# Two small reorderings in a two-block transformer kernel: where the short weight tile of the second output half stands, and when ScalarE splits the third weight tile of the convolutional FFN

## The chip, the cores and the metric

The kernel runs on one core of a Trainium2 chip. The metric is the device time of one execution in microseconds (us); lower is better. TensorE (PE in the profile) multiplies matrices, VectorE (DVE), ScalarE (ACT) and GpSimd (POOL) work on vectors, and SyncE (SP) issues the loads of the weights. Each engine runs its own instruction list in order and meets the others through semaphores.

## The reference, cut to what matters

The reference is two blocks of two layers each on 512 tokens (the first block also carries 256 context tokens in its first layer), in float32. The change touches the down projections of all four feed-forward networks, and the start of the two convolutional ones. Cut to these:

```
_swiglu(h, w_gate, w_up, w_down) = (silu(h @ w_gate) * (h @ w_up)) @ w_down   # first block, 2 layers

def conv_ffn(h, w_up, conv_w, conv_b, w_down):                                # second block, 2 layers
    u = h @ w_up
    u = sum(conv_w[2 - n] * shift(u, n) for n in range(3)) + conv_b           # along the tokens
    gate, up = split(u, 2, axis=-1)
    return (silu(gate) * up) @ w_down
```

The hidden width is 2816, that is 22 blocks of 128, and w_down is 2816 x 1024.

## The kernel before

**How a float32 product is made.** Each factor is held as a high part in the fp32r format and a low part, the rest of it. A product is three matmuls of 128x128 by 128x512 (`mm3`, lines 233 to 235): high by high, high by low, low by high.

**Weight tiles.** All weights pass through one numbered sequence of tiles. SyncE loads tile t into one of two raw buffers as soon as the low part of tile t-2 is made (line 394). ScalarE casts it to the high part (`ScalarLane.tile`, line 345; "hi" below), once TensorE has given back the buffer of tile t-2 (the key "used"). VectorE then makes the low part (`VectorLane.tile`, line 264; "lo"). Each call of `tile()` on ScalarE or VectorE makes sure that the tiles up to one ahead of TensorE's are made. Where the calls stand in the engines' own lists is written out by hand.

**Down projection.** `pe_out` computes the 1024 output columns in two halves of 512, half 0 over all 22 blocks and then half 1. `out_chunks` cuts each half into pieces of at most four blocks, so there are twelve chunks, numbered 0 to 11; 0 to 5 are half 0, 6 to 11 half 1. A chunk is one weight tile (4 blocks: 128x2048 values, 2 blocks: 128x1024). Half 0 is cut 4, 4, 4, 4, 4, 2, and half 1 is cut 4, 4, 2, 4, 4, 4. From the third chunk on TensorE takes one token tile after the other (nt of them: 6 in `down0`, 4 in `down1`, `cf_out0` and `cf_out1`), and for each the blocks of the chunk. So a chunk of n blocks is 3 x n x nt matmuls.

The activations of a chunk are split too: `act_chunk` copies each block of it to its high part (line 345, into rx), `dve_chunk` makes the low part (line 335), one block behind. TensorE waits for each block of the chunk.

VectorE's list, in `dve_out`, is for chunk c: the lo of tile c+1, the activations of chunk c+1, and, if c is the last chunk of a half, the outputs of that half from PSUM, token tile by token tile. So at the switch of the halves it is: lo of tile 6, activations of chunk 6, **outputs of half 0**, lo of tile 7, activations of chunk 7, lo of tile 8, and so on. In `down0` and `down1` an output is three operations (multiply by the gate at line 264, add the scaled residual at 274, statistics at 298); in `cf_out0` and `cf_out1` it is one addition (264). In `cf_out0` ScalarE also squares and sums the four outputs of half 0 (`act_flow_sums`), between the activations of chunk 6 and the hi of tile 7.

`down1` takes its last two chunks (10 and 11) interleaved by token tiles; this is the same in both kernels.

**Start of the convolutional FFN.** The up projection has 44 column tiles of 128 (n = 0 to 43), two per weight tile. Tiles n = 0 to 3 (weight tiles 0 and 1 of the stage) are computed by `pe_feat_halves`, first for tokens 0 to 255 and then for tokens 256 to 511, so all four end within a short stretch; TensorE then goes on with n = 4 and weight tile 2. For each n ScalarE copies the result from PSUM (line 345), VectorE makes three convolution operations on it (lines 270, 274, 274), and for the gate part (n = 0, 1, 4, 5, ...) ScalarE applies Silu (line 341). VectorE's list is: convolutions of n = 0 and 1, lo of weight tile 2, convolutions of n = 2 and 3, lo of weight tile 3. ScalarE's list before the change is: copy 0, Silu 0, copy 1, **hi of weight tile 2**, Silu 1, copy 2, copy 3, hi of weight tile 3.

Of the kernel before, what the change touches and what calls it, by code (L numbers as in the profile page):

```python
# [741 lines left out]

def out_chunks(Kn):


    cut = sorted({*range(0, min(Kn, 9), 4), *range(Kn, 7, -4)})
    return [(0, k0, min(4, Kn - k0)) for k0 in range(0, Kn, 4)] + [(1, i, j - i) for i, j in zip(cut, cut[1:])]


# [9 lines left out]
def out_order(Kn, nt, late):  # L759


    chunks = out_chunks(Kn)
    order = []
    for c, (h, k0, kn) in enumerate(chunks[:-2] if late else chunks):
        order += ([(c, k, t) for k in range(kn) for t in range(nt)] if c < 2 and h == 0 else
                  [(c, k, t) for t in range(nt) for k in range(kn)])
    if late:
        end = len(chunks)
        order += [(c, k, t) for ts in [(0, 1)] + [(t,) for t in range(2, nt)] for c in (end - 2, end - 1) for t in ts
                  for k in range(chunks[c][2])]  # L770
    return order


def pe_out(p, K, tag, W, Kn, nt, ready=None, between=(), chunks=False, turn=None, late=None):


    between, cut, ms, bs = dict(between), out_chunks(Kn), {}, {}
    order = out_order(Kn, nt, late)
    for i, (c, k, t) in enumerate(order):
# [32 lines left out]
def act_chunk(a, K, tag, c, Kn, nt, src, ready):  # L812
    h, k0, kn = out_chunks(Kn)[c]
    places = len(chunk_places(nt))
    if c >= places:
        a.wait_ge(*K.at(tag + "_used", c - places))
    for k in range(kn):
        a.wait_ge(*K.at(*ready, k0 + k))
        a.cp(chunk_parts(K, c, nt)[0][:, k, 0:nt * 128], src[:, k0 + k, 0:nt * 128]).then_inc(
            *a.sig((tag + "_chunk_hi", c, k)))  # L820
# [2655 lines left out]
def cf_out(K):  # L3476
    return K.mem(W1, 11264).rearrange("p (k n) -> p k n", n=512)
# [6 lines left out]
def cf_raw(K, n):  # L3484
    return K.mem(CF + 700 + n % 4 * 514, 514)


def cf_acc(K, n):
    return K.mem(CF + 2760 + n % 8 * 512, 512)


def cf_tiles():

    return [(f2 * 4 + part * 2 + f, part, f2 * 2 + f) for f2 in range(11) for part in range(2) for f in range(2)]
# [38 lines left out]
def act_conv_ffn(a, K, l):  # L3533
    a.wait_ge(*K.at("cf_edge", l))
    for n, part, ft in cf_tiles():
        if n % 2 == 0 and n > 2:
            a.tile()
        if n == 40:
            act_chunk(a, K, f"cf_out{l}", 0, 22, 4, cf_out(K), ("cf_GT", l))
        a.wait_ge(*K.at("cf", l, n))  # L3540
        if n >= 4:
            a.wait_ge(*K.at("cf_conv", l, n - 4))
        a.cp(cf_raw(K, n)[:, 2:514], K.ps("cf", l, n)[:, :]).then_inc(*a.sig(("cf_raw", l, n)))
        a.free("cf", l, n)
        if n == 1:
            a.tile()
        if part == 0:
            a.wait_ge(*K.at("cf_conv", l, n))
            a.act(cf_acc(K, n), cf_acc(K, n), ACT.Silu).then_inc(*a.sig(("cf_silu", l, n)))
# [593 lines left out]
def act_program(a, K):  # L4143
# [58 lines left out]
    yield "x0"  # L4202
    act_flow_halves(a, K, "nf0", K_FFN)
    act_conv_ffn(a, K, 0)
    first, second = act_flow_sums(a, K, "cf_out0", "nhg")
    act_out(a, K, "cf_out0", 22, 4, cf_out(K), ("cf_GT", 0), {5: first, 11: second}, 1)
# [8 lines left out]
    yield "x1"  # L4215
    act_flow_halves(a, K, "nf1", K_FFN + 8)
    act_conv_ffn(a, K, 1)
    act_out(a, K, "cf_out1", 22, 4, cf_out(K), ("cf_GT", 1), made=1)

# [227 lines left out]
```

## Time and profile before

| | |
|---|---|
| time, median of 3 runs | 4284.06 us (4283.25 to 4290.72) |
| the profiled execution | 4283.25 us, its span 4281.0 us |
| PE busy | 3910.1 us, 91% of the span |
| DVE busy | 2099.3 us, 49% |
| ACT busy | 1607.7 us, 38% |
| POOL busy | 561.9 us, 13% |
| mean granted clock of TensorE | 0.953 of full |

Times inside the execution are counted from the start of its span. A matmul's busy time in the profile overlaps that of the next one; the work that it costs is the distance between two starts. In the timeline, the bracket at the end of a row is the idle time of the engine just before the instruction and who ended it.

### The profile page before, as it was taken

Reading aid. Unit: us, or ns where it says so; the run is one execution under the profiler, and the core shown is the slowest. Engines: PE = TensorE matmul, PEld = TensorE weight load, DVE = VectorE, ACT = ScalarE, POOL = GpSimd, SP = SyncE. Lnnn points to the kernel's source line nnn. Section 1 sums busy time; section 2 is a strip of 40 time slices with the busy share of each in tenths; the row PEclk is TensorE's granted clock in tenths of the full one; section 3 lists DMA queues with packets and bytes.
Section 4 is the critical chain, followed back from the end, with each engine's and each line's share of the span. In section 5 each row is a group of like instructions: output and inputs, shape, how many; then the busy total and the mean of one; then the engine's idle time right before and its main releaser. Section 6 shows DMA issues by size and latency. Waiting matters only on the chain.

```text
span 4281.0 us, 67439 instructions
## 1 busy us (share of the span) xinstructions
PE 3910.1 (91%) x28266; PEld 3214.2 (75%) x28266; DVE 2099.3 (49%) x3022; ACT 1607.7 (38%) x2639; POOL 561.9 (13%) x628
## 2 busy tenths in 40 slices
PE   6978897878999998988899889989999998889999
PEld 4866685766888775756688776678888888678887
DVE  3545454656211363267423663554665428545564
ACT  3333333333111233155323335644334336544333
POOL 0035303642000001002100000000220003000220
PEclk8978898888999999999899999999999999999999
DMA  4234433131221121102232230131323230322232
GB/s 155 82 130 140 152 96 115 35 101 48 69 69 60 54 84 61 55 11 76 84 99 94 74 84 20 52 118 51 99 92 102 89 116 5 121 69 72 97 101 86
DMA packets 248535, 355.08 MB, mean 83 GB/s; under 512 B 9300, under 2 KB 158503, under 8 KB 247847
## 3 DMA queue, kind: packets, MB, share of 16 engines
q1 hardware_dynamic: 233840, 300.49, 21.7%
q0 software_dynamic: 13840, 50.11, 3.7%
q8 instruction: 222, 3.64, 0.4%
q14 instruction: 83, 0.67, 0.1%
q10 hardware_dynamic: 550, 0.17, 0.0%
HBM read 336.50 MB, written 14.24 MB: 82 GB/s over the span
## 4 chain that ended last, share of the span: by engine, by line
PE 76%; DVE 12%; ACT 7%; issue 2%; POOL 2%; DMA 1%; ACTq 0%; DVEq 0%; SPq 0%; POOLq 0%
PE psum L233 20%; PE psum L234 20%; PE psum L235 20%; PE psum L230 14%; ACT arena L341 3%; DVE arena L264 3%; PE psum L239 2%; DVE arena L274 2%; DVE rw L264 2%; DVE rx L335 2%; ACT arena L345 1%; POOL arena L379 1%; DVE arena L278 1%; ACT rw L345 1%; ACT rx L345 1%
## 5 line engine op out<-in xcount | busy, mean ns | idle before, releaser
L233 PE MATMUL psum<-rx,rw 128*128 128x512 f32 (+2 forms) x2864 | 1046.3, 365 | 53.7 <-DVE rx L335 27.7
L234 PE MATMUL psum<-rx,rw 128*128 128x512 f32 (+2 forms) x2864 | 1026.8, 359 | 0.0
L235 PE MATMUL psum<-rx,rw 128*128 128x512 f32 (+2 forms) x2864 | 1026.1, 358 | 0.0
L230 PE MATMUL psum<-arena 32*32 32x32 f32 (+10 forms) x12982 | 808.4, 257 | 159.3 <-ACT arena L345 64.5
L264 DVE TENSOR_TENSOR rw<-arena,rw 128x2048 fp32r<-128x2048 f32 (+2 forms) x239 | 537.6, 2249 | 829.8 <-ACT rw L345 824.1
L230 PEld LDWEIGHTS psum<-arena 32*32 32x32 f32 (+5 forms) x12982 | 612.8, 141 | 335.6 <-issue 118.6
L345 ACT ACTIVATE rw<-arena 128x2048 fp32r<-128x2048 f32 (+2 forms) x239 | 448.1, 1875 | 755.5 <-PE psum L235 728.9
L233 PE MATMUL psum<-rw,rx 128*128 128x512 f32 (+1 forms) x1720 | 682.0, 397 | 43.9 <-DVE rx L335 26.9
L234 PE MATMUL psum<-rw,rx 128*128 128x512 f32 (+1 forms) x1720 | 673.0, 391 | 0.0
L235 PE MATMUL psum<-rw,rx 128*128 128x512 f32 (+1 forms) x1720 | 672.7, 391 | 0.0
L233 PEld LDWEIGHTS psum<-rx,rw 128*128 128x128 f32 (+1 forms) x2864 | 548.5, 192 | 155.1 <-DVE rx L335 41.2
L234 PEld LDWEIGHTS psum<-rx,rw 128*128 128x128 f32 (+1 forms) x2864 | 549.9, 192 | 80.2 <-issue 4.1
L235 PEld LDWEIGHTS psum<-rx,rw 128*128 128x128 f32 (+1 forms) x2864 | 548.4, 191 | 78.5
L345 ACT ACTIVATE arena<-psum 128x512 f32<-128x512 f32 (+6 forms) x675 | 314.4, 466 | 757.3 <-PE psum L235 401.4
L379 POOL TENSOR_TENSOR arena<-arena 128x512 f32<-128x512 f32 (+5 forms) x300 | 420.2, 1401 | 969.5 <-DVE arena L274 389.5
L341 ACT ACTIVATE arena<-arena 128x512 f32<-128x512 f32 (+11 forms) x476 | 249.5, 524 | 471.5 <-DVE arena L274 219.3
L233 PEld LDWEIGHTS psum<-rw,rx 128*128 128x128 f32 x1720 | 327.7, 191 | 125.3 <-DVE rx L335 39.2
L235 PEld LDWEIGHTS psum<-rw,rx 128*128 128x128 f32 x1720 | 327.2, 190 | 68.4
L234 PEld LDWEIGHTS psum<-rw,rx 128*128 128x128 f32 x1720 | 327.8, 191 | 64.4
L274 DVE SCALAR_TENSOR_TENSOR arena<-arena 128x512 f32<-128x512 f32 (+8 forms) x481 | 353.9, 736 | 44.5 <-ACT arena L341 27.9
L264 DVE TENSOR_TENSOR arena<-arena,psum 128x512 f32<-128x512 f32 (+3 forms) x308 | 151.8, 493 | 311.5 <-PE psum L235 205.1
L239 PE MATMUL psum<-arena 128*128 128x128 f32 (+2 forms) x1284 | 196.0, 291 | 102.8 <-DVE arena L264 33.7
(71 smaller groups left out, 2092.5 us busy)
## 6 DMA issues: line engine op xcount, KB each, us to landing
arena<-in_ffn_w_up SPq DMA_DIRECT2D x66, 1024.0 KB, 5.1
arena<-in_ada_w SPq DMA_DIRECT2D x48, 1024.0 KB, 5.3
arena<-in_ffn_w_down SPq DMA_DIRECT2D x40, 1024.0 KB, 5.0
arena<-in_ffn_w_gate SPq DMA_DIRECT2D x22, 1024.0 KB, 5.2
arena<-in_dn_w_in SPq DMA_DIRECT2D x32, 512.0 KB, 5.4
arena<-in_xa_w_kv SPq DMA_DIRECT2D x16, 1024.0 KB, 5.0
arena<-in_hgrn_w_in SPq DMA_DIRECT2D x16, 1024.0 KB, 5.5
arena<-in_da_w_in SPq DMA_DIRECT2D x12, 1024.0 KB, 5.2
```

The source lines that it names most:

```text
L230: return self.e.matmul(out, l, r, start=start, stop=stop)
L233: self.e.matmul(out, l[0], r[0], start=start, stop=False)
L234: self.e.matmul(out, l[0], r[1], start=False, stop=False)
L235: return self.e.matmul(out, l[1], r[0], start=False, stop=stop)
L239: return self.e.transpose(out, a, self.K.ident[0:k, 0:k])
L264: return self.e.tensor_tensor(out, a, b, op)
L274: return self.e.scalar_tensor_tensor(out=out, in0=a, scalar=s, in1=b, op0=op0, op1=op1)
L278: return self.e.tensor_reduce(out, a, AX.X, op)
L335: return self.e.tensor_tensor(dst[1], src, dst[0].bitcast(F32), SUB)
L341: return self.e.activation(out, a, f, **kw)
L345: return self.e.activation(out, a, ACT.Copy, **kw)
L379: return self.e.tensor_tensor(out, a, b, op)
```

## The change

Two edits:

1. In `out_chunks` half 1 is cut 2, 4, 4, 4, 4, 4 instead of 4, 4, 2, 4, 4, 4. The number of chunks (twelve) and all other sizes stay. The short chunk of half 0 (chunk 5) is now followed by the short chunk of half 1 (chunk 6). For the other users of this function, with 8 blocks, both versions give 4, 4.
2. In ScalarE's list at the start of both convolutional FFNs the hi of weight tile 2 moves from behind copy 1 to behind Silu 1: copy 0, Silu 0, copy 1, Silu 1, **hi of weight tile 2**, copy 2, copy 3, hi of weight tile 3. VectorE's and TensorE's lists stay.

```diff
 def out_chunks(Kn):
-    cut = sorted({*range(0, min(Kn, 9), 4), *range(Kn, 7, -4)})
+    cut = [0] + list(range(Kn % 4 or 4, Kn + 1, 4))
     return [(0, k0, min(4, Kn - k0)) for k0 in range(0, Kn, 4)] + [(1, i, j - i) for i, j in zip(cut, cut[1:])]
...
 def act_conv_ffn(a, K, l):
     a.wait_ge(*K.at("cf_edge", l))
     for n, part, ft in cf_tiles():
-        if n % 2 == 0 and n > 2:
+        if n and n % 2 == 0:
             a.tile()
...
         a.cp(cf_raw(K, n)[:, 2:514], K.ps("cf", l, n)[:, :]).then_inc(*a.sig(("cf_raw", l, n)))
         a.free("cf", l, n)
-        if n == 1:
-            a.tile()
         if part == 0:
             a.wait_ge(*K.at("cf_conv", l, n))
             a.act(cf_acc(K, n), cf_acc(K, n), ACT.Silu).then_inc(*a.sig(("cf_silu", l, n)))
```

## Rows read from the trace of the kernel before

**Rows 1.** The page's shares of the chain that ended last, by engine.

```profile
PE 76%; DVE 12%; ACT 7%; issue 2%; POOL 2%; DMA 1%; ACTq 0%; DVEq 0%; SPq 0%; POOLq 0%
```

**Rows 2.** ACT timeline in `down0`, hi of tiles 6, 8, 11, 12: start us, us.

```profile
1496.64 1.92 ACT L345 ACTIVATE rw<-arena 128x2048 fp32r<-128x2048 f32 x1 [13.38 <-PE psum L235]
...
1521.12 1.06 ACT L345 ACTIVATE rw<-arena 128x1024 fp32r<-128x1024 f32 x1 [10.88 <-PE psum L235]
...
1564.66 1.92 ACT L345 ACTIVATE rw<-arena 128x2048 fp32r<-128x2048 f32 x1 [10.88 <-PE psum L235]
...
1580.98 1.92 ACT L345 ACTIVATE rw<-arena 128x2048 fp32r<-128x2048 f32 x1 [10.88 <-PE psum L235]
```

**Rows 3.** DVE timeline in `down0`: lo 5, activations of chunks 5 and 6, then lo 7.

```profile
1481.41 1.23 DVE L264 TENSOR_TENSOR rw<-arena,rw 128x1024 fp32r<-128x1024 f32 x1 [8.92 <-ACT rw L345]
1482.74 2.02 DVE L335 TENSOR_TENSOR rx<-arena,rx 128x768 fp32r<-128x768 f32 x2
...
1500.98 4.15 DVE L335 TENSOR_TENSOR rx<-arena,rx 128x768 fp32r<-128x768 f32 x4
...
1518.91 2.29 DVE L264 TENSOR_TENSOR rw<-arena,rw 128x2048 fp32r<-128x2048 f32 x1
```

**Rows 4.** Timeline of PE in `down0`, the first matmul of chunk 7.

```profile
1522.41 0.47 PE L233 MATMUL psum<-rw,rx 128*128 128x512 f32 x1 [1.39 <-DVE rx L335]
```

**Rows 5.** Timeline of ACT in `down1`, hi of tiles 6, 10 and 11.

```profile
2376.75 1.92 ACT L345 ACTIVATE rw<-arena 128x2048 fp32r<-128x2048 f32 x1 [8.37 <-PE psum L235]
...
2414.97 1.92 ACT L345 ACTIVATE rw<-arena 128x2048 fp32r<-128x2048 f32 x1 [0.86 <-PE psum L235]
...
2426.23 1.92 ACT L345 ACTIVATE rw<-arena 128x2048 fp32r<-128x2048 f32 x1 [6.68 <-PE psum L235]
```

**Rows 6.** DVE timeline in `down1`: activations of chunks 5 and 6, then lo 7.

```profile
2368.29 1.49 DVE L335 TENSOR_TENSOR rx<-arena,rx 128x512 fp32r<-128x512 f32 x2
...
2381.09 3.08 DVE L335 TENSOR_TENSOR rx<-arena,rx 128x512 fp32r<-128x512 f32 x4
...
2393.40 2.29 DVE L264 TENSOR_TENSOR rw<-arena,rw 128x2048 fp32r<-128x2048 f32 x1
```

**Rows 7.** Timeline of PE in `down1`, the first matmul of chunk 7.

```profile
2396.64 0.47 PE L233 MATMUL psum<-rw,rx 128*128 128x512 f32 x1 [3.26 <-DVE rx L335]
```

**Rows 8.** Timeline of ACT in `cf_out0`, hi of tiles 6 and 7.

```profile
3279.17 1.92 ACT L345 ACTIVATE rw<-arena 128x2048 fp32r<-128x2048 f32 x1 [8.37 <-PE psum L235]
...
3290.71 1.92 ACT L345 ACTIVATE rw<-arena 128x2048 fp32r<-128x2048 f32 x1
```

**Rows 9.** Timeline of PE in `cf_out0`, the first matmul of chunk 7.

```profile
3295.89 0.47 PE L233 MATMUL psum<-rw,rx 128*128 128x512 f32 x1
```

**Rows 10.** Timeline of ACT in `cf_out1`, hi of tiles 6 and 11.

```profile
4210.85 1.92 ACT L345 ACTIVATE rw<-arena 128x2048 fp32r<-128x2048 f32 x1 [8.37 <-PE psum L235]
...
4255.49 1.92 ACT L345 ACTIVATE rw<-arena 128x2048 fp32r<-128x2048 f32 x1 [7.04 <-PE psum L235]
```

**Rows 11.** Stretches for PE: us, PE busy (matmuls), granted clock, DMA share, GB/s.

```profile
1406.50:1417.90 11.40, 6.06 (x14) 0.70 0.27 93
2393.30:2401.00 7.70, 4.44 (x13) 0.78 0.42 136
3345.60:3351.60 6.00, 3.75 (x26) 1.00 0.01 3
```

**Rows 12.** Timeline of ACT at the first convolutional FFN's start.

```profile
3002.27 1.92 ACT L345 ACTIVATE rw<-arena 128x2048 fp32r<-128x2048 f32 x1
3004.37 0.63 ACT L341 ACTIVATE arena<-arena 128x512 f32<-128x512 f32 x1 [0.18 <-DVE arena L274]
```

**Rows 13.** Timeline of DVE there, lo of weight tile 2.

```profile
3004.44 2.29 DVE L264 TENSOR_TENSOR rw<-arena,rw 128x2048 fp32r<-128x2048 f32 x1
```

**Rows 14.** Timeline of PE there, last matmul of n = 3, first of n = 4.

```profile
3006.39 0.28 PE L235 MATMUL psum<-rx,rw 128*128 128x256 f32 x1
3006.79 0.50 PE L233 MATMUL psum<-rx,rw 128*128 128x512 f32 x1
```

## The prediction

> **What bounds the kernel now.** I read the page first: PE is busy 91% of the span and carries 76% of the chain that ended last [rows 1]. Neither edit adds or removes a matmul, a cast or a load, so only PE's waits can change. Then I read the timelines of ACT, DVE and PE side by side at the five kinds of place that the edits touch. The useful clock is ACT's hi cast: the hi of tile c+2 starts when TensorE gives back the buffer of chunk c, so its start marks the end of chunk c whenever the row names PE as releaser. I count tiles within a stage, as the chunks.
>
> The unit is a chunk. In `down0` two such marks are 1580.98 - 1564.66 = 16.32 us apart [rows 2]: four blocks by six token tiles by three matmuls, 72 in all, so 0.227 us a matmul. A block then costs 4.08 us of PE in `down0` and 0.227 x 12 = 2.72 us in the other three. The short chunk gives 8.16 us of cover in `down0` and 5.44 us elsewhere.
>
> From the end of chunk 4 to the end of chunk 9 both kernels work off 16 blocks. In `down0` this takes 1564.66 - 1496.64 = 68.02 us against 65.28, so 2.74 us are lost [rows 2]. In `down1`: 2426.23 - 2376.75 = 49.48 against 43.52, 5.96 lost [rows 5]. In `cf_out1`: 44.64 against 43.52, 1.12 lost [rows 10].
>
> The large loss is in chunk 7. DVE has just taken the outputs of half 0. In `down0` that is all between 1505.1, where the activations of chunk 6 end, and 1518.91, where the lo of tile 7 begins: 13.8 us for six outputs, 2.3 us each [rows 3]. The first matmul of chunk 7 starts at 1522.41, after 1.39 us of idleness put down to DVE [rows 4]. In `down1` it is four outputs, and PE idles 3.26 us [rows 7].
>
> **The change, part by part: the short chunk in place 6.** Two things move at the switch.
>
> *DVE's chain moves up.* Tile 6 and its activations are halved. In `down0` the hi takes 1.06 us instead of 1.92 [rows 2], the lo 1.23 instead of 2.29, the activations 2.02 instead of 4.15 [rows 3]. DVE has no gap from there to the lo of tile 7, so that comes 0.86 + 1.06 + 2.13 = 4.05 us earlier. In the stages with four token tiles the activations take 1.49 instead of 3.08 [rows 6], so it is 3.51 us earlier. The outputs can follow: PE finishes a token tile of chunk 5 every 1.36 us, DVE takes one every 2.3.
>
> *PE's cover shrinks* by 8.16 us, respectively 5.44. So PE waits longer before chunk 7, and what comes later has two blocks more to do. The first matmul of chunk 7 comes 4.05 (3.51) us earlier, and 8.16 (5.44) us of matmuls are moved behind it.
>
> `down0`: 8.16 - 4.05 = +4.11. The wait grows from 1.39 to about 5.4 us: chunk 6 ends at 1496.64 + 8.16 + 8.16 = 1512.96, the first matmul comes at 1522.41 - 4.05 = 1518.36. What does so long a pause do to the clock? At 1406.5 PE had paused 11.40 - 6.06 = 5.3 us and then ran 14 matmuls in 6.06 us, at a granted clock of 0.70 over the stretch. At full clock that is 3.17, so 2.9 us were lost. After the 3.26 us of `down1`, 13 matmuls took 4.44 us, so 1.5 lost. After 2.2 us at 3345.6 the clock stayed at 1.00 [rows 11]. So +2.9 here. Against that, chunk 7 now also loses about 1.1 us block by block, because DVE makes a block's low part in 4.15 / 4 = 1.04 us [rows 3] while PE uses it in 0.68; at the lower of the two clock levels, 1.2 GHz, PE takes 1.28, and this wait goes. Sum: 4.11 + 2.9 - 1.1 = **+5.9**.
>
> Here a rule stands beside the rows. The Trainium skill, page "TensorE: Matmul & The Clock Gate", section "Why this matters for your kernels", says that pauses between bursts of matmuls put the array back to its half rate, and that one should keep them short. The two longer pauses agree; the 2.2 us pause shows that not every pause does it here. Without the rule and its rows, `down0` would be +3.0; if every new pause paid, the sum would be that of the clock rival below.
>
> `down1`: 5.44 - 3.51 = +1.93. The pause becomes 2396.64 - 3.51 - (2376.75 + 10.88) = 5.5 us, so the clock costs 2.9 instead of 1.5, +1.4. The chunk after the short one loses 2426.23 - 2414.97 - 10.88 = 0.38 us now [rows 5], since its activations come late; behind a long chunk that goes. **+2.9**.
>
> `cf_out0`: an output is one addition, but ACT squares all four before the hi of tile 7, at 3290.71 [rows 8]. These follow the outputs, so that hi moves up by the same 3.51, and the first matmul from 3295.89 [rows 9] to 3292.38. Chunk 6 ends at 3279.17 + 10.88 = 3290.05: a pause of 2.3 us, close to the one that left the clock alone. 1.93 - 0.37 (chunk 9, as in `down1`) = **+1.6**, or +3.1 if the clock drops after all.
>
> `cf_out1`: outputs without squares, one operation of about 0.77 us each (a third of 2.3). DVE comes to them some 4 us after the end of chunk 4 (1.06 + 1.23 + 1.49 us and the gaps between), at 4214.9, and the last, ready at 4216.3, is taken by 4218. Tile 7's hi, released by the end of chunk 5 at 4216.3, is just done then. The lo and the first blocks are then in time as they are for chunk 6 now. Of the 1.12 us lost [rows 10], the share of the one transition from a short to a long chunk stays, 0.38: **-0.7**.
>
> Sum of this edit: 5.9 + 2.9 + 1.6 - 0.7 = **+9.7 us**. Bounds: if the longer pauses cost the clock no more than 1.5 each, 2.8 less; if it drops in `cf_out0`, 1.5 more. The loads aren't late: raw tile 8 is asked for when the lo of tile 6 is done, which is earlier than now.
>
> **The hi of weight tile 2 behind Silu 1.** Now ACT casts at 3002.27 for 1.92 us, then waits 0.18 us for DVE's convolution 1 and applies Silu at 3004.37 [rows 12]. DVE starts the lo at 3004.44 [rows 13], and PE's first matmul of n = 4 starts at 3006.79, right at its end. The last one of n = 3 started at 3006.39 [rows 14]. So PE has no slack on this lo: it ends 0.06 us before PE uses it.
>
> After: Silu 1 still starts at 3004.37, since it waits for DVE. The cast begins behind it, at 3004.37 + 0.63 + 0.09 = 3005.09, and ends at 3007.01. The lo starts at 3007.03 instead of 3004.44, **+2.6 us**, and PE follows. Queued behind the cast on ACT are copies 2 and 3; they free PSUM and feed DVE, which is by then still at the lo. The lo of weight tile 3 goes back by as much, but PE needs it only 10.9 us after it starts n = 4. The same order stands in the second convolutional FFN: together **+5.2**. The new pause is about 2.7 us, between the 2.2 that left the clock alone and the 3.26 that cost 1.5 [rows 11]. I take none, for it is nearer to the first, and keep 1.5 each for the range. What would hide this edit is a PE still busy with n = 3 for 2.6 us more; there is none.
>
> **Sum.** 9.7 + 5.2 = +14.9 us. Against the profiled execution, 4281.0 us of span and 4283.25 with what lies around it, this gives 4298.2. The median of the runs is 0.8 above that execution, so I give 4298.5. A run of this kernel can tell about 0.2%, 8.6 us.
>
> **The rivals.**
>
> *The clock drops after the three middling pauses too* (`cf_out0`, both FFN starts): +1.5 each, 4303. For it: the 3.26 us pause did it, and 2.7 isn't far. Against: 2.2 us didn't, in an otherwise busy stretch. 17 in 100.
>
> *The outputs of half 0 don't hold tile 7 up.* If DVE's part from chunk 5 to the lo of tile 7 moved up with PE, by 8.16 (5.44) us, the pause would not grow, and the small transition losses (0.4 at chunk 6, 0.38 at chunk 9) would go: -2.3 in this edit, and with the other +2.9, 4287, no change that can be told. It decides from where the outputs start as soon as PE finishes them and end within a short chunk; 13.8 us of outputs against 8.16 us of cover speak against it. 7 in 100. This is the case that is not slower.
>
> *The cast's move is hidden.* If another engine's work held the first matmul of n = 4 anyway, only the first edit counts: 4293. Against: PE's wait ends 0.06 us after this very lo. 6 in 100.
>
> *The short chunk helps more than it costs*, because long chunks at 8 to 11 keep PE fed: every loss of those chunks is 0.38 us, so this gains at most 1 us. It is in the sum; a faster kernel would need something unseen. 2 in 100.
>
> **How the numbers follow.** The forecast has 62 in 100 (4296 to 4301 by its own bounds), the clock 17, the outputs 7, the cast 6, a gain 2, and 6 for what I don't see, mostly above. The range 4292 to 4304 leaves out the outputs, the gain and part of the rest. Slower by over 0.2% is above 4292.6: the forecast, the clock, half of the cast's case and most of the unseen, 0.86. Within 0.2%: 0.12. Faster: 0.02.
>
> **What would show it.** In `down0` and `down1`, idleness of about 5.4 us put down to DVE before chunk 7, and then 14 to 15 matmuls at 0.43 us from start to start; in `cf_out0` 2.3 us without them; in `cf_out1` no pause at chunk 7 beyond a few tenths. From the end of chunk 4 to that of chunk 9, 8.6, 8.9, 3.0 and 0.4 us lost. At both FFN starts, a Silu ahead of the cast and about 2.7 us of pause before n = 4. Everything else should only be shifted. The prediction is wrong if DVE starts the lo of tile 7 elsewhere than 4.05 or 3.51 us earlier, or if a shifted stage meets other pauses of the clock.

## The result, and the profile after

The changed kernel takes 4309.4 us (median of 7 runs, 4294.20 to 4322.24) against 4283.62 (7 runs, 4280.73 to 4290.72): the ratio estimated from the runs is 1.0052, with a 95% interval of 1.0034 to 1.0070 (the two medians alone give 1.0060). It is slower, as forecast, but by 25.8 us where 14.9 were forecast, and outside the range of 4292 to 4304 us. Its seven runs spread over 28 us, those of the kernel before over 10. Ratios leave out one execution, of the changed kernel with `down1` split (below), that took 10413 us where its other eleven took 4290.63 to 4303.73.

| | before | after |
|---|---|---|
| the profiled execution | 4283.25 us | 4309.93 us |
| its span | 4281.0 us | 4307.7 us |
| PE busy | 3910.1 us | 3920.8 us |
| DVE busy | 2099.3 us | 2097.2 us |
| ACT busy | 1607.7 us | 1606.8 us |
| mean granted clock | 0.953 | 0.949 |

**The switch of the halves in `down0`.** The hi casts of tiles 6, 8 and 11, the marks of the ends of chunks 4, 6 and 9, answering to [rows 2]:

```profile
1498.19 1.06 ACT L345 ACTIVATE rw<-arena 128x1024 fp32r<-128x1024 f32 x1 [13.38 <-PE psum L235]
...
1514.51 1.91 ACT L345 ACTIVATE rw<-arena 128x2048 fp32r<-128x2048 f32 x1 [2.72 <-PE psum L235]
...
1571.70 1.92 ACT L345 ACTIVATE rw<-arena 128x2048 fp32r<-128x2048 f32 x1 [10.88 <-PE psum L235]
```

Sixteen blocks take 1571.70 - 1498.19 = 73.51 us, so 8.23 are lost where 2.74 were and 8.6 were forecast. VectorE in the same stretch, from its first output of half 0 to the lo of tile 7, for [rows 3]:

```profile
1502.77 0.69 DVE L264 TENSOR_TENSOR arena<-psum,arena 128x512 f32<-128x512 f32 x1
...
1516.42 2.29 DVE L264 TENSOR_TENSOR rw<-arena,rw 128x2048 fp32r<-128x2048 f32 x1
```

The lo comes 1516.42 - 1498.19 = 18.23 us after the end of chunk 4; it was 22.27. That is 4.04 earlier, the forecast's 4.05. But PE was done with chunk 6 after 16.3, at 1514.51. The last matmul of chunk 6 and the first of chunk 7, for [rows 4]:

```profile
1514.04 0.39 PE L235 MATMUL psum<-rw,rx 128*128 128x512 f32 x1
1519.92 0.77 PE L233 MATMUL psum<-rw,rx 128*128 128x512 f32 x1 [5.49 <-DVE rx L335]
```

The idleness grew from 1.39 to 5.49 us.

**`down1`, `cf_out0`, `cf_out1`.** The first matmul of chunk 7 in `down1` and in `cf_out0`, for [rows 7, 9]:

```profile
2401.36 0.77 PE L233 MATMUL psum<-rw,rx 128*128 128x512 f32 x1 [5.58 <-DVE rx L335]
...
3312.83 0.47 PE L233 MATMUL psum<-rw,rx 128*128 128x512 f32 x1 [2.41 <-DVE rx L335]
```

The hi of tiles 6 and 11 in `down1`, `cf_out0` and `cf_out1`, for [rows 5, 8, 10]:

```profile
2384.99 1.06 ACT L345 ACTIVATE rw<-arena 128x1024 fp32r<-128x1024 f32 x1 [8.37 <-PE psum L235]
...
2436.46 1.92 ACT L345 ACTIVATE rw<-arena 128x2048 fp32r<-128x2048 f32 x1 [6.30 <-PE psum L235]
...
3299.63 1.06 ACT L345 ACTIVATE rw<-arena 128x1024 fp32r<-128x1024 f32 x1 [8.37 <-PE psum L235]
...
3347.48 1.92 ACT L345 ACTIVATE rw<-arena 128x2048 fp32r<-128x2048 f32 x1 [6.30 <-PE psum L235]
...
4238.27 1.06 ACT L345 ACTIVATE rw<-arena 128x1024 fp32r<-128x1024 f32 x1 [8.37 <-PE psum L235]
...
4282.15 1.92 ACT L345 ACTIVATE rw<-arena 128x2048 fp32r<-128x2048 f32 x1 [6.30 <-PE psum L235]
```

Against 43.52 us of matmuls these pairs are 51.47, 47.85 and 43.88 apart, so 7.95, 4.33 and 0.36 us are lost; forecast were 8.9, 3.0 and 0.4.

**The start of the first convolutional FFN**, for [rows 12 to 14]: Silu 1 and then the hi of weight tile 2 on ScalarE, its lo on VectorE, and on PE the last matmul of n = 3 and the first three of n = 4.

```profile
3019.43 0.63 ACT L341 ACTIVATE arena<-arena 128x512 f32<-128x512 f32 x1 [2.19 <-DVE arena L274]
3020.15 1.92 ACT L345 ACTIVATE rw<-arena 128x2048 fp32r<-128x2048 f32 x1
...
3022.10 2.29 DVE L264 TENSOR_TENSOR rw<-arena,rw 128x2048 fp32r<-128x2048 f32 x1 [2.71 <-ACT rw L345]
...
3021.45 0.28 PE L235 MATMUL psum<-rx,rw 128*128 128x256 f32 x1
3024.45 0.80 PE L233 MATMUL psum<-rx,rw 128*128 128x512 f32 x1 [2.71 <-DVE rw L264]
3025.04 0.63 PE L234 MATMUL psum<-rx,rw 128*128 128x512 f32 x1
3025.47 0.63 PE L235 MATMUL psum<-rx,rw 128*128 128x512 f32 x1
```

The pause is the 2.7 us of the forecast. But the second and third matmul behind it last 0.63 us and start 0.43 apart, where a matmul at the full clock takes 0.227. Stretches of PE in this trace (us, busy and matmuls, granted clock, DMA share, GB/s): behind the pauses of `down0`, `down1`, `cf_out0` and both FFN starts.

```profile
1514.50:1526.50 12.00, 6.58 (x18) 0.72 0.27 89
2395.80:2407.50 11.70, 6.14 (x18) 0.71 0.26 92
3310.40:3318.00 7.60, 5.19 (x17) 0.78 0.44 139
3021.80:3031.50 9.70, 7.05 (x19) 0.65 0.34 108
3961.50:3971.00 9.50, 6.78 (x23) 0.82 0.35 112
```

The clock fell in all five places, also in the three behind pauses of 2.4 to 2.7 us. The 19 matmuls at 3021.8 took 7.05 us against 19 x 0.227 = 4.3, so 2.7 us went there. By the same count the stretch in `down0` lost 2.5 us, the one in `down1` 2.05, the one in `cf_out0` 1.3 and the one at the second FFN start 1.6.

**Where the 26.7 us of the span went.** Every weight tile has one lo on VectorE, and both traces hold the same 238 of them in the same order. The difference of the starts of the same lo in two traces says how late the second runs there; how much it grows in a stage is what that stage lost. For this and the experiments' traces (times are those of the kernel before; "both" is the changed kernel, "again" a second trace of the same kernel):

| stage, us | before again | chunk | chunk again | cast | both | both again |
|---|---|---|---|---|---|---|
| 0 to 1342 | +0.3 | -1.9 | +2.5 | -0.6 | +1.7 | +5.6 |
| `down0`, 1481 to 1567 | 0.0 | +5.45 | +5.47 | 0.0 | +5.49 | +5.51 |
| 1567 to 2367 | -0.2 | +1.1 | +1.2 | -0.2 | +1.2 | +1.1 |
| `down1`, 2367 to 2428 | 0.0 | +2.00 | +2.00 | 0.0 | +1.99 | +2.00 |
| 2428 to 2545 | +0.1 | -1.04 | -1.04 | +0.1 | -1.06 | -1.06 |
| 2545 to 2601 | 0.0 | +2.67 | +2.69 | 0.0 | +4.24 | +4.28 |
| 2601 to 2983 | 0.0 | -0.1 | -0.1 | +0.1 | +1.65 | +1.69 |
| FFN start, 2983 to 3075 | 0.0 | 0.0 | 0.0 | +2.59 | +5.40 | +2.63 |
| `cf_out0`, 3269 to 3326 | 0.0 | +1.54 | +1.54 | 0.0 | +2.93 | +2.87 |
| 3326 to 3915 | -0.1 | +2.68 | +2.67 | +0.5 | -0.2 | +1.2 |
| FFN start, 3915 to 4007 | 0.0 | 0.0 | 0.0 | +3.93 | +4.21 | +3.91 |
| `cf_out1`, 4201 to 4257 | 0.0 | -0.73 | -0.76 | 0.0 | -0.76 | -0.73 |

The stages left out, from 1342 to 1481, 3075 to 3269 and 4007 to 4201, differ by 0.1 us or less. In the trace after, the edited places hold 5.49 + 1.99 + 2.93 - 0.76 = 9.65 us for the chunks and 5.40 + 4.21 = 9.61 for the cast. The other 5.8 us behind 1342 lie in stages whose instructions are the same, and 1.7 ahead of it, where every trace differs.

### The profile page after: what moved, and what is told of

The parts are those of the page before. It is cut to its first block, busy times and chain, and to the rows that moved or that the text cites. A ratio compares the mean times of both kernels' runs of the same rounds, so it can differ in the third digit from the quotient of the medians.

```text
span 4307.7 us, 67439 instructions
## 1 busy us (share of the span) xinstructions
PE 3920.8 (91%) x28266; PEld 3229.7 (75%) x28266; DVE 2097.2 (49%) x3022; ACT 1606.8 (37%) x2639; POOL 561.3 (13%) x628
## 4 chain that ended last, share of the span: by engine, by line
PE 76%; DVE 12%; ACT 7%; POOL 2%; issue 2%; DMA 1%; ACTq 0%; DVEq 0%; SPq 0%; POOLq 0%
PE psum L233 20%; PE psum L234 20%; PE psum L235 20%; PE psum L230 13%; ACT arena L341 3%; DVE arena L264 3%; PE psum L239 3%; DVE rw L264 2%; DVE arena L274 2%; POOL arena L379 1%; ACT arena L345 1%; DVE rx L335 1%; ACT rw L345 1%; DVE arena L278 1%; DVE arena L270 1%
```

## The experiments

Each experiment ran beside the kernel before on the same chip; the medians of that kernel were 4282.21 us for the first four, 4284.36 for the next four and 4284.89 for the last four. The ratios go by these.

### The kernel before, once more

No edit.

> The kernel before, unchanged, for a second trace of it. The theory that the 7 us which the changed kernel lost outside the five edited places are chance of one execution expects differences of a few us between two traces of this same kernel, at the same kinds of place (pauses of PE where the granted clock is once 0.5 and once 1.0). The theory that they come from the change expects the two traces of this kernel to agree within 1 us in every stage. Time 4281 to 4290.

4285.05 us, ratio 1.0009 (1.0000 to 1.0018). Between the two traces of this kernel no stage from 1158 us on differs by more than 0.3 us, and the stretches of lower clock fall in the same places. Ahead of 1158 us they differ by up to 2 us. So the theory that the losses outside the edited places are chance of one execution fails for this kernel: its stages behind 1158 us repeat themselves, and its two traces differ in the first quarter alone.

### Each edit alone

```diff
 def out_chunks(Kn):
-    cut = sorted({*range(0, min(Kn, 9), 4), *range(Kn, 7, -4)})
+    cut = [0] + list(range(Kn % 4 or 4, Kn + 1, 4))
```

> The short chunk of half 1 in first place, the cast where it was. Theory A (each place pays for itself): down0 +5.5, down1 +2.2, cf_out0 +1.6 to +3.2, cf_out1 -0.5, so +9 to +10.5 us, a time of about 4294. Theory B (the loss elsewhere comes from this edit, by what it does to the stages behind it): +16 or more, 4300. My prediction's own figure for this edit was +9.7.

4296.71 us, ratio 1.0034 (1.0021 to 1.0046). In place it loses 5.45 + 2.00 + 1.54 - 0.73 = 8.3 us, as theory A has it, but another 5.3 elsewhere (table). Theory B expected such a loss, and a larger whole, 16 us or more; it was 14.5.

```diff
 def act_conv_ffn(a, K, l):
-        if n % 2 == 0 and n > 2:
+        if n and n % 2 == 0:
             a.tile()
...
-        if n == 1:
-            a.tile()
```

> The hi of weight tile 2 behind Silu 1 at both convolutional FFN starts, the chunks as before. My prediction's figure: 2.6 us at each, +5.2, 4289. If the clock falls to its lower level after the new pause of about 2.7 us, +1.5 to +2.9 more at each, so up to +10, 4294. A second trace shows whether it falls every time. Nothing ahead of 3004 us should move beyond what two traces of the kernel before differ by.

4289.74 us, ratio 1.0014 (1.0005 to 1.0023). In the trace the two FFN starts lose 2.59 and 3.93 us. PE's stretches behind the two pauses:

```profile
3006.10:3014.10 8.00, 5.34 (x23) 1.00 0.40 131
3940.90:3950.90 10.00, 7.32 (x26) 0.83 0.33 107
```

The timeline shows both pauses at 2.72 us. Behind the first the clock stayed at its higher level, and the start cost the bare 2.6; behind the second it fell.

### Both again

> The changed kernel again, for a second trace and more times. If the two edits simply add: the excess of the chunk edit plus that of the cast edit, about +20, 4303, and the five edited places show +5.5, +2.2, +5.4, +3.2, +4.1, -0.5 again where the clock falls in the same places. If the clock's part is chance, the second trace has other places at the lower clock, and the times spread by more than those of the kernel before (10 us).

4304.80 us, ratio 1.0047 (1.0034 to 1.0061). The two edits' excesses, 14.5 and 7.5 us, add up to 22.0; both together have 22.6 here. The same FFN start that cost 5.40 us in the first trace costs 2.63 in this one; its two stretches:

```profile
3025.50:3036.00 10.50, 7.78 (x36) 1.00 0.31 100
3963.80:3973.80 10.00, 7.28 (x29) 0.83 0.33 107
```

So a pause of 2.7 us can go either way even in one kernel. `cf_out0`, whose pause is 2.4, lost the clock's part in both traces of this kernel (+2.9) and in neither of the chunk edit alone (+1.5). The other traces with both edits or with the chunk edit bear this out: `cf_out0` lost +2.9 with `down1` split and +1.5 with the chunk edit and a delay (both below), so the clock's part in three of six traces. The two FFN starts lost it in five of eight places: the first in one trace of four, the second in all four. The pauses of 5.5 us in the changed kernel and the chunk kernel lost it every time.

The expectation had two theories, and each is met in part. The excesses add up; the four places of the chunk edit repeat themselves to 0.1 us and the second FFN start to 0.3, but the first FFN start doesn't.

### The lo of tile 7 between the outputs, in the kernel before

```diff
 def dve_out(...):
+    early, first = (5, 4 if nt > 4 else 2) if src is not None else (-9, 0)
...
-            v.tile()
+            if c - 1 != early:
+                v.tile()
...
             for t in range(nt):
+                if c == early and t == first:
+                    v.tile()
+                    dve_chunk(v, K, tag, made, Kn, nt, src)
+                    made += 1
...
-    act_out(a, K, "cf_out0", 22, 4, cf_out(K), ("cf_GT", 0), {5: first, 11: second}, 1)
+    act_out(a, K, "cf_out0", 22, 4, cf_out(K), ("cf_GT", 0), {6: first, 11: second}, 1)
```

> The kernel before (half 1 cut 4, 4, 2, ...), but VectorE makes the lo and the activations of chunk 7 in the middle of the outputs of half 0: after four of six in down0, after two of four in the others; ScalarE squares cf_out0's outputs behind the hi of tile 7. Theory A (VectorE's outputs hold tile 7 up, PE's cover decides): the losses of chunk 7 go, 2.7 us in down0, 5.2 in down1, 0.7 in cf_out0, so -8.6 us, about 4274, with no idleness of PE put down to DVE before chunk 7. Rival (tile 7 waits for its load or its hi): the pauses stay, 4282.

4278.46 us, ratio 0.9985 (0.9976 to 0.9993): faster than both kernels. `down0` gains 2.74 us, `down1` 5.21 and `cf_out0` 0.65, as expected to the tenth. PE's stretches across the ends of chunk 6 in `down0` and `down1`:

```profile
1510.00:1535.00 25.00, 25.00 (x112) 1.00 0.24 85
2378.00:2410.00 32.00, 32.00 (x142) 1.00 0.25 82
```

No pause, and the full clock. So VectorE's outputs held tile 7 up in `down0` and `down1`, not its load or its hi. Of the expected 8.6 us the runs show 5.9, the trace 7.2: again other stages moved by a few us.

### The same in `down1` alone, in the changed kernel

```diff
+    early, first = (5, 1) if tag == "down1" else (-9, 0)
```

with the same lines in `dve_out`, and both edits of the change.

> The changed kernel, and in down1 alone VectorE makes the lo and the activations of chunk 7 after the first output of half 0 instead of after the fourth. Theory A: the pause of 5.5 us and the stretch at the lower clock behind it go in down1, and only a few tenths stay, so down1 takes 7.5 to 8.5 us less than in the changed kernel, and the time is about 8 us below it, 4297 to 4301. Rival (it is the short chunk itself, or the load of tile 7, not the outputs): down1 keeps its pause.

4296.79 us, ratio 1.0028 (1.0019 to 1.0036). The view of waits for PE in `down1` has one line (us in total, times, longest):

```profile
PE psum L233 <- DVE rx L335: 1.0, 1, 1.0
```

The pause falls from 5.58 to 1.0 us, and the stage is 4.05 us faster than the kernel before instead of 1.99 slower: 6.0 us less (7.5 to 8.5 were expected). With the outputs out of the way, the short chunk in that place costs `down1` 1.2 us (4.05 gained here, 5.21 by the split without it). `down0`, not touched, loses its 5.4.

### Filling the pause at the FFN starts

```diff
 def pe_conv_ffn(p, K, l):
     for n, part, ft in order[4:]:
+        if n == 4:
+            b = p.bank("cf", l, n)
+            for i in range(FILL):
+                p.mm(b[:, 0:128], K.ident, K.ident)
...
-        b = p.bank("cf", l, n)
+        if n != 4:
+            b = p.bank("cf", l, n)
```

on top of the cast edit, FILL = 22.

> The cast edit alone, with 22 small matmuls (128x128 of the identity, some 0.12 us each) into the PSUM bank of n = 4, which the first real matmul there overwrites, put where TensorE waits for weight tile 2 at both FFN starts. Theory A (the pause costs 2.6 us, and what the traces show above that is the lower clock level after it): each start costs 2.6 to 2.9 us over the kernel before and never 3.9 or 5.4, the granted clock stays at 1.00 there, and the time is 4282 + 5.5 = 4288. Rival (the excess over 2.6 is another engine being late): the starts still cost 3.9 or more in the trace.

4291.82 us, ratio 1.0019 (1.0010 to 1.0028). The filling and the first real matmul behind it:

```profile
3004.20 5.07 PE L230 MATMUL psum<-arena 128*128 128x128 f32 x44
3009.03 0.47 PE L233 MATMUL psum<-rx,rw 128*128 128x512 f32 x1
```

A float32 matmul shows as two, and the 22 took 4.83 us: they outlasted the pause, and each start costs 4.54 us. This run decides nothing.

FILL = 11:

> As e6_cast_filled, with 11 filling matmuls instead of 22: those 22 took 4.83 us (0.22 each) and outlasted the pause by 2.0 us, so that run didn't tell. Theory A: 11 take 2.4 us, fill the pause of 2.72, and each FFN start costs 2.6 to 2.8 us over the kernel before, also the second, which cost 3.9 in both traces without them; so about +5.4 in the trace. Rival: the second start still costs 3.9.

4287.79 us, ratio 1.0009 (1.0000 to 1.0018). The filling and the first real matmul in the timeline of PE:

```profile
3009.41 2.62 PE L230 MATMUL psum<-arena 128*128 128x128 f32 x22
3012.30 0.50 PE L233 MATMUL psum<-rx,rw 128*128 128x512 f32 x1 [0.27 <-DVE rw L264]
```

and PE's stretches at the two starts:

```profile
3009.00:3019.00 10.00, 9.73 (x56) 1.00 0.32 105
3942.00:3952.00 10.00, 9.74 (x64) 1.00 0.32 107
```

The starts cost 2.62 and 2.61 us. The second cost 3.91 to 4.23 in all four traces without the filling, and has lost what exceeded the wait. The first shows nothing here, since it cost the bare 2.6 in three of the four traces without the filling too. So the late lo costs 2.6 us and the rest, 1.3 to 2.8 us where it shows, is the lower clock behind an idle PE; the filling shows this at the second start, and the stretch at 3021.8 with its 2.7 us at the first. From 1342 us on this trace is 5.7 us longer than the kernel before; the medians differ by 2.9 us, with an interval of 0 to 7.7, and can't tell 5.7 from the 7.0 of the cast edit's trace.

### The chunk edit once more

> The chunk edit alone once more, for a second trace and a tighter median. Theory A: down0 +5.5, down1 +2.0, cf_out0 +1.5 to +2.9, cf_out1 -0.7 as in the first trace, together 8.3 to 9.7, and what lies elsewhere differs from trace to trace with the stretches of lower clock: the median comes down from +14.5 towards +10. Theory B (a steady loss elsewhere, of the stages behind the edit): the stage from 2545 to 2601 us and the one around 3670 again cost 2.7 and 3.5 us more than in the kernel before, and the median stays at +14.

4299.27 us, ratio 1.0036 (1.0024 to 1.0048). The median did not come down (14.9 us above the kernel before), and from 1342 us on the trace is the first one's again, to 0.03 us in each row of the table. What is lost in stages that nobody edited is steady, as theory B has it. But what is lost there? The stage from 2545 us, in five traces, answers it. PE's stretch in the kernel before:

```profile
2546.00:2602.00 56.00, 51.92 (x240) 0.92 0.17 57
```

The same stretch in its second trace:

```profile
2546.10:2602.10 56.00, 52.00 (x240) 0.92 0.17 57
```

In the first trace of the chunk edit:

```profile
2551.50:2610.20 58.70, 54.60 (x239) 0.88 0.16 54
```

In its second trace:

```profile
2556.00:2614.70 58.70, 54.64 (x240) 0.88 0.16 54
```

And in the changed kernel's first trace:

```profile
2555.10:2615.40 60.30, 56.18 (x240) 0.85 0.16 53
```

The idle time is the same in all five, 56.00 - 51.92 = 4.1 us in the first and 4.0 to 4.1 in the others. The same 240 matmuls take 51.9, 54.6 or 56.2, as the granted clock is 0.92, 0.88 or 0.85.

The table holds one thing more. The chunk kernel and the changed kernel have the same instructions up to the first FFN start at 2983 us, and they come to 2545 us equally late, 7.5 us behind the kernel before counted from 1342. Yet each loses its own amount from there to 2983, in both of its traces: 2.6 us in the chunk kernel, 5.9 and 6.0 in the changed one. Nothing here explains that.

### A bare delay

In the kernel before, and (the last) in the chunk edit:

```diff
 def pe_out(...):
             bs[t, h] = p.bank(tag, t, h)
+        if tag == "down1" and i == 0:
+            for _ in range(SHIFT):
+                p.mm(bs[t, h][:, 0:128], K.ident, K.ident)
```

> The kernel before, delayed at one place: 5 small matmuls (1.1 us) in front of the first matmul of down1, into a PSUM bank that it overwrites. Nothing else changes. Theory B2 (where a stretch of lower clock falls in the stages behind depends on when they run, so a delay costs more or less than itself): the stage from 2545 to 2601 us costs another amount than in the kernel before, by 1 to 4 us, with the same waits and a different granted clock. Rival (the chunk edit's loss there has a cause of its own in the edit): this stage is unchanged, and the trace is 1.1 us longer.

4282.54 us, ratio 0.9995 (0.9987 to 1.0004). The delay of 1.1 us is seen at 2367 us; but `down1` then takes 0.15 us less, the stage from 2428 to 2545 takes 0.98 less, and from 1342 us to the end the kernel is 0.50 us faster than without the delay. The stage that I had named, 2545 to 2601, stayed as it was (+0.05), so the expectation of theory B2 for it was missed.

> As e9_shift5, with 10 matmuls (2.2 us). Theory B2: again another cost of the stages behind, and not in proportion to the delay. Rival: the trace is 2.2 us longer and every stage else as before.

4287.02 us, ratio 1.0004 (0.9995 to 1.0013). 2.2 us of delay, 3.20 at the end: `down1` lost 0.95 more. Its pause is the same 3.26 us, but the lower clock behind it lasts longer. PE's stretch of 11.7 us around that pause in the kernel before:

```profile
2393.30:2405.00 11.70, 8.44 (x31) 0.85 0.54 179
```

and with the delay:

```profile
2398.20:2409.90 11.70, 8.44 (x26) 0.71 0.56 181
```

The same busy time holds 31 matmuls or 26. The stage from 2545 to 2601 again stayed as it was (+0.10).

> The chunk edit alone, with 11 small matmuls (2.4 us) in front of down1. Theory B2: the stage from 2545 to 2601, which lost 2.7 us in both traces of the chunk edit, loses another amount, near nothing if the delay brings it back to where the kernel before had it, so that the whole is no longer than without the delay. Rival: it still loses 2.7 and the time is 2.4 us above e1_chunk_only, some 4300.

4297.80 us, ratio 1.0027 (1.0015 to 1.0038). PE in the stage from 2545 us:

```profile
2554.50:2611.00 56.50, 51.80 (x240) 0.92 0.17 56
```

It is back at the kernel before: -0.25 us instead of +2.7, at a clock of 0.92. So 2.4 us of useless matmuls, at 2327 us and so some 225 us earlier, gave 2.9 back there, and from 1342 us on the kernel is at 13.2 us of excess with them, 13.5 without. The chunk edit is still in this kernel and its loss in this stage is gone, so the edit's own waits don't cause it; a shift in time ahead of the stage does away with it. The arrival at the stage alone doesn't settle the amount: the kernel before with 1.1 and 2.2 us of delay lost nothing there, and the chunk kernel and the changed kernel arrive alike and lose 2.7 and 4.2. And the delay didn't touch the other loss of this kind: the stage from 3326 to 3915 costs +2.68 here, as in both traces of the chunk edit.

## Why the prediction was wrong

The direction, both waits and their places were right; the size was not. By its own steps:

- **DVE's chain moves up by 4.05 and 3.51 us, PE's cover shrinks by 8.16 and 5.44**: right. The pauses are 5.49 and 5.58 us (5.4 and 5.5 forecast), in `cf_out0` 2.41 (2.3), in `cf_out1` none. That the outputs of half 0 hold tile 7 up is shown by the two splits.
- **The clock behind the long pauses, 2.9 us each**: too much. The stretches at the lower clock lost 2.5 us in `down0` and 2.05 in `down1`, so `down0` lost 5.49 us more (5.9 forecast) and `down1` 1.99 (2.9).
- **`cf_out0` without the clock, +1.6**: +1.54 in both traces of the chunk edit alone, +2.9 in both of the changed kernel. **`cf_out1`, -0.7**: -0.73 to -0.76. The sum for the chunk edit in its own places, 9.7, was met, 8.3 to 9.65, but in the changed kernel by luck: the two long pauses cost 1.3 us less than forecast and `cf_out0` 1.3 more.
- **The cast, +2.6 us at each start**: the wait is right, 2.59 to 2.63 where the clock holds, and shown by the filled pause. "I take none, for it is nearer to the first" is the first step that failed. The clock fell behind one or both of these pauses in each of the four unfilled traces with this edit, and the two starts together cost 6.5 us (cast alone), 9.6 and 6.5 (both edits) and 6.9 (with `down1` split), against 5.2. The rival with the clock at all three middling pauses, to which I gave 17 in 100, is what the first trace shows, at about the forecast size: 1.4 us in `cf_out0`, 2.8 and 1.6 at the starts, 5.8 together against 4.5.
- **"Everything else should only be shifted"** is the second step that failed, and the larger one for the range. Stages without an edit lost 5.8 us behind 1342 in the first trace of the changed kernel, 7.2 in the second, and 5.3 with the chunk edit alone. They hold the same instructions and, in the stage from 2545 to 2601, the same idle time; what differs there is the granted clock, 0.85 to 0.88 instead of 0.92. The forecast named this only among what would make it wrong, without a price.

The Trainium skill's rule, in "TensorE: Matmul & The Clock Gate", section "Why this matters for your kernels", that pauses between bursts cost the full rate, agrees with the pauses of 5.5 us in the changed kernel and the chunk kernel without exception. For those of 2.4 to 2.7 us the traces here show both outcomes, with the same wait.

The sum for the first trace: 14.9 forecast, +4.4 at the FFN starts, about 0 in the chunks' places, +5.8 elsewhere, +1.7 ahead of 1342 us, which gives 26.7 with rounding. The second set of runs of the changed kernel, 4304.80 us, is above the range as well. What remains open: of the unedited stages only the one from 2545 to 2601 was examined for its waits and its clock, and moved by a delay. That the +2.7 us between 3326 and 3915 in the chunk kernel has the same cause is not shown. There it goes with `cf_out0`: in the three traces in which `cf_out0` lost 1.5 us the stage behind lost 2.7, in the three in which it lost 2.9 the stage lost between -0.6 and +1.2. Nor is it shown why a stage's clock repeats itself between two executions, though the two differ by up to 4 us in when they come to it.

## What to carry to other kernels

Where one engine prepares the next weight tile behind a block of output work, the matmuls of the tile in flight are the cover: place the largest tile there, or put the preparation in the midst of the outputs; that took out 2.7 and 5.2 us here. A pause of TensorE is to be priced as wait plus clock, and a pause somewhat below one that has lowered the clock gets about an even chance, not none: here the clock fell behind 8 of 14 such pauses of 2.4 to 2.7 us. And a forecast of a few us in a kernel with many ragged stages needs room for the stages behind the edit: here stages with the same instructions changed by -1 to +4 us each, 5 to 7 us in all, and a bare delay took 2.9 us back in one of them.

## What was not expected of the hardware

Two executions of one kernel agree stage by stage to 0.03 us over the last 2900 us (both traces of the chunk edit), with the granted clock low in the same places, though they enter that part 4.4 us apart. The two traces of the kernel before agree to 0.2 us a stage; those of the changed kernel agree to 0.3 us but for one FFN start (2.8 us) and the stage from 3326 to 3915 (1.4 us). A delay of 1.1 us made the rest 1.6 us faster, one of 2.2 us made it 1.0 us slower. Most of the scatter between traces of one kernel lies in the first 1342 us, at whose end the traces, all with the same instructions so far, lie between -2.4 and +7.1 us of the first trace of the kernel before.
